# Moving single VectorE, ScalarE and TensorE instructions in a two-block fp32 transformer kernel

## The reference, cut to what matters

```
def rmsnorm(x, g):
    y = xf * lax.rsqrt(jnp.mean(xf * xf, axis=-1, keepdims=True) + EPS)
    return (y * g.astype(jnp.float32)).astype(x.dtype)

# first block: pooled and forgetting attention, memory attention, then
    gu = jnp.einsum('bsd,df->bsf', hn, w_gate_up[l])
    act = jax.nn.silu(gu[..., :D_FF]) * gu[..., D_FF:]
    h = h + jnp.einsum('bsf,fd->bsd', act, w_down[l])

# second block, two layers: feed-forward, short convolution or differential attention, feed-forward
    gate, up = jnp.split(x @ w_gu, 2, axis=-1)
    return (jax.nn.silu(gate) * up) @ w_down
    h = h + 0.5 * rmsnorm_2(swiglu(rmsnorm_2(h, g[0]), ffn_w_gu[l, 0], ffn_w_down[l, 0]), g[1])
    h = h + 0.5 * rmsnorm_2(swiglu(rmsnorm_2(h, g[4]), ffn_w_gu[l, 1], ffn_w_down[l, 1]), g[5])
```

## Time and profile before

| | |
|---|---|
| Time, median of three | 1270.5 us |
| Profiled execution: its time, its span | 1271.37 us, 1269.6 us |
| Granted TensorE clock, mean | 0.999 |
| TensorE matmuls busy | 1253.5 us, 99% |
| VectorE busy | 1042.7 us, 82% |
| ScalarE busy | 804.0 us, 63% |
| GpSimd busy | 192.4 us, 15% |

### The profile page before, as it was taken

How to read it: one execution, slowest core, us unless ns; L and a number is a source line. 1 busy time by engine, 2 the same in 40 slices (tenths; PEclk the granted TensorE clock), 3 DMA queues, 4 the chain that set the end, 5 groups by cost and what they waited for, 6 DMA issues and landing times.

```text
span 1269.6 us, 15538 instructions
## 1 busy us (share of the span) xinstructions
PE 1253.5 (99%) x5897; PEld 1028.9 (81%) x5897; DVE 1042.7 (82%) x1035; ACT 804.0 (63%) x986; POOL 192.4 (15%) x224
## 2 busy tenths in 40 slices
PE   9999999999999999999999999999999999999998
PEld 7888878888888878788778888788888877788886
DVE  6766689999799996767899997999977568999984
ACT  6674576665576664645766664766656466766662
POOL 6142130110001100102201101111001003301100
PEclk9999999999999999999999999999999999999999
DMA  9537498997649955568979978389745535999931
GB/s 333 174 100 231 133 313 254 268 270 248 201 151 255 269 168 180 188 226 215 320 249 245 271 251 255 116 237 274 219 166 173 184 125 168 315 286 262 266 135 44
DMA packets 143002, 277.32 MB, mean 218 GB/s; under 512 B 8992, under 2 KB 39896, under 8 KB 142928
## 3 DMA queue, kind: packets, MB, share of 16 engines
q1 hardware_dynamic: 120192, 229.67, 51.6%
q0 software_dynamic: 22288, 45.54, 19.7%
q10 hardware_dynamic: 448, 1.12, 0.2%
HBM read 275.24 MB, written 1.05 MB: 218 GB/s over the span
## 4 chain that ended last, share of the span: by engine, by line
PE 77%; DVE 12%; issue 4%; ACT 3%; DMA 3%; POOL 0%; DVEq 0%; SPq 0%; ACTq 0%
PE B L2102 14%; PE B L2104 14%; PE B L2103 14%; DVE w_lo L1359 7%; PE B L2558 6%; PE B L2560 6%; PE B L2559 6%; PE T L2102 3%; PE T L2104 3%; PE T L2103 3%; DMA VD<-in_ffn_w_gu 2%; DVE VD L1378 1%; DMA Z<-in_ffn_w_gu 1%; ACT w_hi L1082 1%; ACT w_hi L768 1%
## 5 line engine op out<-in xcount | busy, mean ns | idle before, releaser
L1359 DVE TENSOR_TENSOR w_lo<-w_raw,w_hi 128x2048 fp32r<-128x2048 f32 x129 | 296.5, 2299 | 87.5 <-ACT w_hi L768 87.2
L768 ACT ACTIVATE w_hi<-w_raw 128x2048 fp32r<-128x2048 f32 x129 | 247.1, 1918 | 102.7 <-PE B L2560 60.3
L2102 PE MATMUL B<-w_hi,xt_lo 128*128 128x512 f32 x652 | 260.5, 400 | 5.1 <-DVE w_lo L1359 2.1
L2104 PE MATMUL B<-w_hi,xt_hi 128*128 128x512 f32 x652 | 254.7, 391 | 0.0
L2103 PE MATMUL B<-w_lo,xt_hi 128*128 128x512 f32 x652 | 254.0, 390 | 0.0
L2558 PE MATMUL B<-w_hi,act_lo 128*128 128x512 f32 x440 | 172.5, 392 | 0.8 <-DVE w_lo L1359 0.4
L2560 PE MATMUL B<-w_hi,act_hi 128*128 128x512 f32 x440 | 171.4, 390 | 0.0
L2559 PE MATMUL B<-w_lo,act_hi 128*128 128x512 f32 x440 | 171.3, 389 | 0.0
L2102 PEld LDWEIGHTS B<-w_hi,xt_lo 128*128 128x128 f32 x652 | 122.4, 188 | 36.1 <-issue 6.2
L2104 PEld LDWEIGHTS B<-w_hi,xt_hi 128*128 128x128 f32 x652 | 122.4, 188 | 26.4
L2103 PEld LDWEIGHTS B<-w_lo,xt_hi 128*128 128x128 f32 x652 | 122.6, 188 | 23.3
(11 more groups left out here) (330 smaller groups left out, 2110.0 us busy)
## 6 DMA issues: line engine op xcount, KB each, us to landing
w_raw<-in_ffn_w_down SPq DMA_DIRECT2D x88, 512.0 KB, 5.8
Z<-in_ffn_w_gu SPq DMA_DIRECT2D x64, 512.0 KB, 8.1
w_raw<-in_ffn_w_gu SPq DMA_DIRECT2D x48, 512.0 KB, 5.2
nat<-in_ffn_w_gu SPq DMA_DIRECT2D x32, 512.0 KB, 7.8
QT<-in_ffn_w_gu SPq DMA_DIRECT2D x32, 512.0 KB, 7.0
Z<-in_ffn_w_gu POOLq DMA_DIRECT2D x32, 512.0 KB, 8.8
w_raw<-in_conv_w_in SPq DMA_DIRECT2D x24, 512.0 KB, 4.7
w_raw<-in_w_down SPq DMA_DIRECT2D x22, 512.0 KB, 6.6
```

The costliest lines, as they stand in the source:

```text
L768: act.activation(whi[home(u)][:, :], raw[slot][:, :], ACT.Copy).then_inc(w_hi, 1)
L1359: dve.tensor_tensor(wlo[home(u)][:, :], src, whi[home(u)][:, :].bitcast(F32), ALU.subtract).then_inc(w_lo, 1)
L2102: pe.matmul(bank[:, :], lo[:, k, x], whi[s][:, c], start=first, stop=False, skip_group_check=more)
L2104: return pe.matmul(bank[:, :], hi[:, k, x], whi[s][:, c], start=False, stop=last, skip_group_check=more)
```

## The change

The same instructions run with the same operands. Only their places in the lists of their engines move:

```
@@ ScalarE, ffn: gate_of(0) ahead of the high part of the sums of x
                 block("P1", 0)
+                act.wait_ge(rstd, 2 * ST[stat] + 2)
+                gate_of(0, u0 + OP["N0b", 0], PAIR[0] if f else F0)
                 act.wait_ge(sx_ok, f + 1)
                 act.wait_ge(w_used, u0 + OP["N0b", 0] + 1)
                 act.activation(yhi[:, :, :], xsum, ACT.Copy).then_inc(sx_hi, 1)
-                act.wait_ge(rstd, 2 * ST[stat] + 2)
-                gate_of(0, u0 + OP["N0b", 0], PAIR[0] if f else F0)
                 block("P2", 0)
@@ VectorE, first block
-            split_at(7)
             dve.wait_ge(c_hi, 1)
             low = slice(64, CK)
             dve.tensor_tensor(cT[low, :], B[3][low, 0:S], cT[low, :].bitcast(F32), ALU.subtract).then_inc(c_out, 1)
+            split_at(7)
@@ VectorE, ffn: start of a layer, square 0
-                if f == 0:
-                    total = x_total(reader)
-                else:
+                if f:
                     update(0)
...
+                weights("N1b")
+                if f == 0:
+                    total = x_total(reader)
                 x_sums(total)
-                weights("N1b")
-                block("P1", 0)
                 dve.wait_ge(rstd, 2 * ST[stat] + 2)
                 act_of(0, PAIR[0] if f else F0)
+                block("P1", 0)
                 dve.wait_ge(sx_hi, f + 1)
...
                 block("P3", 0)
+                block("P7", 0)
                 weight_sum("T4", f, 0)
-                block("P7", 0)
                 weights("D0")
...
                 result("C12", 0)
+                act_out(1)
                 weight_sum("T1", f, 1)
-                act_out(1)
                 result("C11", 0)
@@ VectorE, ffn: squares 1 to 3
                     block("P6", p)
-                    if p not in ADDED_T4:
-                        weight_sum("T4", f, p)
                     block("P3", p)
                     block("P7", p)
                     act_out(2 * p)
                     weights("Da", p - 1)
+                    if p not in ADDED_T4:
+                        weight_sum("T4", f, p)
                     act_out(2 * p + 1)
...
                     result("C12", p)
+                    weights("Db", p - 1)
                     if p + 1 < SQUARES:
                         weight_sum("T1", f, p + 1)
-                    weights("Db", p - 1)
                     result("C11", p)
...
+                if kv:
+                    kv_round_lo(2)
                 split_at(u0 + FFN_UNITS)
                 if kv:
-                    kv_round_lo(2)
                     kv_round_lo(3)
@@ VectorE, convolution and attention
-            conv_taps(2)
             conv_lo(0)
             conv_lo(1)
+            conv_taps(2)
...
             o_sum(1)
+            o_norm(1)
             heads_lo(0)
-            o_norm(1)
@@ TensorE, end of every ffn
-                down("Db", SQUARES - 1, (lambda: kv_round(2)) if kv else (lambda: None))
+                d, u = down_ready("Db", SQUARES - 1)
+                down_part(d, u, 0, 0)
+                down_part(d, u, 0, 1)
+                if kv:
+                    kv_round(2)
+                down_part(d, u, 1, 0)
                 if kv:
                     kv_round(3)
-                d, u = down_ready("DN2", 0)
-                down_part(d, u, 0, 0).then_inc(tok0_done, 1)
-                down_part(d, u, 0, 1).then_inc(tok0_done, 1)
+                d1, u1 = down_ready("DN2", 0)
+                down_part(d1, u1, 0, 0).then_inc(tok0_done, 1)
+                down_part(d1, u1, 0, 1).then_inc(tok0_done, 1)
+                down_part(d, u, 1, 1).then_inc(w_used, 1)
+                d, u = d1, u1
                 down_part(d, u, 1, 0).then_inc(tok1_half, 1)
@@ TensorE, output product of the differential attention
+            out_heads(0, 4, 1)
             heads_pair(3)
-            for k in (4, 5):
-                out_heads(0, k, 1)
-            pe.wait_ge(ao_lo, 4)
-            for t in range(TOKS):
-                for k in (6, 7):
-                    out_heads(0, k, t)
-            for k in (6, 7):
-                out_heads(1, k, 0)
-            for k in range(4, KD):
+            out_heads(0, 5, 1)
+            out_heads(1, 4, 1)
+            pe.wait_ge(ao_lo, 4)
+            for half in range(2):
+                for k in (6, 7):
+                    out_heads(half, k, 0)
+            for k in (6, 7):
+                out_heads(0, k, 1)
+            for k in (5, 6, 7):
                 out_heads(1, k, 1)
```

## The result

The changed kernel takes 1292.43 us (median of 6 runs, 1292.02 to 1293.69), the kernel before 1271.07 us on the same chip (1270.05 to 1272.24). The ratio is 1.017, 95% interval 1.0157 to 1.0183. The loss is 21.4 us by the medians and 20.6 by the spans (1269.6 and 1290.2). The prediction said +18.0, 1288.5 us.

A forecast was written before the change was run, and what follows sets the result against it. TensorE was taken to bound the kernel (1253.5 of 1269.6 us busy), VectorE close behind. 10.7 + 4.6 + 4.05 - 1.1 + 0.75 - 1.0 = +18.0 us on 1270.5 gave 1288.5 us; 8-in-10 range 1279 to 1295.

The forecast's parts named there:

- T1 behind Db: Two places in each layer: VectorE idles for Db's high part, so P6 starts late; 10.7 us lost in all.
- T1 behind act_out(1): Once in each layer: VectorE's work starts 1.31 us later, waiting for the activations' high part; 4.6 us lost.
- T4 behind P7: Square 0 of each layer: the wait at P7 goes and returns larger at D0; 4.05 us lost.
- T4 behind Da: Square 3: P3's low part no longer stands behind T4; 1.1 us won in layers 1 and 2.
- starts: Start of a layer: N1b's low part ahead of the sums of x; +0.75 us together, bounds -2 and +3.
- the rest: Last key/value turn, first token's sum, forget-gate sums, convolution, o_norm and out_heads: together -1.0 us, between 0 and -3.
- A: Rival, 16%: VectorE's cover larger than read, 15 places in the squares cost half, 9.7 us go; about 1279.
- 0.69 us of cover: VectorE's slack from the end of P6's low part to P6's start; 1.93 us idle less this loses 1.24.
- B: Rival, 9%: transfers late too, T3 landing later after T1; 0.6 us more in each of 15 places, about 1297.
- C: Rival, 5%: TensorE's listed waits (4.2 + 0.51) go and VectorE's new gaps are covered; 1265.5.
- TensorE's list of low-part waits: Sign: longer by some 15 us, at P5 and P6 of squares 1, 2 and 3 and at D0.
- idle ahead of Db's low part: Sign: VectorE idle about 1.9 us there at ten places, ended by ScalarE's L768.

The follow-up runs named there:

- db_only: The kernel before with only T1 moved behind Db's low part (ten places): 1286.47 us, before 1271.26, ratio 1.0115.
- after_T4_cut: The whole change with GpSimd's additions of T4 cut to 16 of 128 partitions: 1291.19 us, before 1271.07, ratio 1.0157.
- dose kernels: The kernel before with one or two unused VectorE sums of 128x512 ahead of T1 at the ten places: 1274.64 and 1281.19 us, before 1270.8.
- act_out_only: The kernel before with only T1 moved behind act_out(1) at square 0 (five places): 1284.81 us, before 1271.26, ratio 1.0106.
- db_T1_cut: The kernel of db_only with T1 in squares 2 and 3 summing 64 of its 2048 columns: 1269.82 us, before 1271.07, ratio 0.9989.

## Why the prediction was right, and where it was off

**T1 behind Db.** Too small by 3.6 us (10.7 against 14.3), and right in mechanism for this move by itself: the working gave 17.56 us from P2 to P6, and eight places of db_only show 17.57 to 17.59, where an idle of 1.89 us costs 1.26. In the changed kernel the close agreement at the first place is in part luck, since another idle, ahead of P4's low part, gives the same time there. Three pieces were missing. I took 0.82 for all four places of layers 1 and 2; with 17.58 against their own 16.64, 16.37, 16.74 and 16.99 the ten places give 11.1. T4's landing adds 2.0 (after_T4_cut). The last 1.1 us is the restart: behind a new stall a stretch of TensorE runs about 0.1 us longer, which I counted at P3 but not here. The step that failed is "the new list holds the same work and starts it at 241.31": it starts when P4's low part is through, and that hangs on a transfer. At all ten places VectorE's idle stands ahead of P4's low part (1.64 to 2.55 us), ended by a high part that waits for T4.

**T1 behind act_out(1), T4 behind P7.** 5.1 and 4.4 for 4.6 and 4.05; the difference is about the restart again. That T1's delay is charged once is right only in company. Alone it costs 13.5, because it pushes T4's landing past the gap at the first Db.

**T4 behind Da, starts, the rest.** -3.2 us in all for -1.35. The parts predicted as small gains were gains. The convolution gave nothing net: 0.3 us won there were given back 20 us later.

**The rivals.** A, that cover halves the loss, fell: every one of the ten places lost more than the working gave it (1.24 us, 0.82 in layers 1 and 2). The 0.69 us of cover ahead of P6 is borne out by db_only; the dose kernels use up the other cover, of 0.54 us, ahead of Db. A's price was also added up wrongly: 9.7 us is half of 20 places (10.7 + 4.6 + 4.05), while half of the 15 named is 7.7 and gives about 1281. B, late transfers, was right in kind but named the wrong one. It had T3 and put the cause at +0.6 in 15 places; it was T4's addition, +2.0 at ten places on top of Db's order, and 7.4 at five in act_out_only. ScalarE waited for Z once, 1.3 us, and TensorE did not notice. C is excluded by db_T1_cut the other way round: the gap is harmless only when 2.1 us of work behind it are gone. Its condition of 0.69 us fits: of 1.89 us of idle in db_only all but 0.63 were lost.

**The signs.** TensorE's list of low-part waits grew by 13.8 us (18.4 from 4.6), said were 15. The idle ahead of Db's low part was foretold for ten places as ended by L768. The view by groups (xcount, busy and mean, idle before) shows otherwise: L768's idle grew by 8 us only, and that ahead of VD's low parts by 18. In square 0 the 1.3 us ahead of P7's low part are there (1.31 to 1.34), ahead of act_lo it is 0.92 to 0.96 instead of 1.2, and P3 of square 3 has no wait. The groups of the changed kernel:

```profile
L1359 DVE TENSOR_TENSOR w_lo<-w_raw,w_hi 128x2048 fp32r<-128x2048 f32 x129 | 296.3, 2299 | 95.6 <-ACT w_hi L768 95.4
L1359 DVE TENSOR_TENSOR w_lo<-VD,w_hi 128x2048 fp32r<-128x2048 f32 x40 | 91.5, 2288 | 20.8 <-ACT w_hi L1082 20.7
```

The same groups of the kernel before:

```profile
L1359 DVE TENSOR_TENSOR w_lo<-w_raw,w_hi 128x2048 fp32r<-128x2048 f32 x129 | 296.5, 2299 | 87.5 <-ACT w_hi L768 87.2
L1359 DVE TENSOR_TENSOR w_lo<-VD,w_hi 128x2048 fp32r<-128x2048 f32 x40 | 91.5, 2287 | 3.0 <-ACT w_hi L1082 3.0
```

What stays open: why T4 takes longer in layer 1 of the kernel before than in the others (11.1 us from issue to high part against 9.9 to 10.2) with the next loads equally far behind it. It was not tried apart.

## What to carry to other kernels

An in-order engine that is almost the bound must not be handed, first, an instruction whose input is not ready, when it has ready work to put in front; compare the idle that this inserts with the cover, from the end of its last product to the start of the consumer, and expect only the difference to be lost. Then follow what each late product releases, transfers above all: a transfer whose issue moves by 1.5 us may land 2.8 us later when others move up behind it. Where two late inputs meet at one place, taking one away shows only how far it stands above the other. Costs of moves on one engine don't add (35 us alone, 24 together), so price them in company, and undo them in company.

## What the runs showed that was not expected

One move of 1.3 us on VectorE cost 1.0 to 1.7 us again some 20 us later in a place that it does not touch, through a transfer of 1 MB whose time from issue to use went from 10.2 to 11.5 us. And the order of two loads of the same size on SyncE's queue, with no other change, took 2.0 us more off the kernel by the medians (ratios 0.9968 and 0.9951, intervals that overlap); P2 to P6 shows 1.1 us of it.
